# In a seven-level state recurrence, the key half of each level is scaled and copied ahead of the level's products

## The chip, the cores and the metric

The kernel runs on one core of a Trainium2 chip. The metric is the device time of one execution in microseconds (us), as the median of several runs. Five engines work side by side, each through its own queue of instructions in order: TensorE (PE, matrix products), VectorE (DVE), ScalarE (ACT), GpSimd (POOL) and SyncE (SP, which issues the loads). They wait for one another through semaphores only.

## The reference

One sequence of 256 tokens with 2048 features goes through two blocks. The first is a gated linear recurrence with input and output projections. The second mixes a convolution branch and a bidirectional gated state recurrence ("hgrn") and ends in an MLP. The change lies in the recurrence of the second block:

```python
def hgrn_chunk_scan(q, k, v, logf, s0):
    ...
    def step(s, xs):
        qc, kc, vc, gc = xs
        a = jnp.cumsum(gc, axis=2)
        a_last = a[:, :, -1:, :]
        inter = jnp.einsum('bhtk,bhkv->bhtv', qc * jnp.exp(a), s)
        diff = a[:, :, :, None, :] - a[:, :, None, :, :]
        decay = jnp.exp(jnp.where(tri[:, :, None], diff, -jnp.inf))
        scores = jnp.einsum('bhtk,bhsk,bhtsk->bhts', qc, kc, decay)
        intra = jnp.einsum('bhts,bhsv->bhtv', scores, vc)
        ...

def hgrn_bidir(q, v, gf, gb, s0f, s0b):
    o_f, s_f = hgrn_chunk_scan(q, gf[1], v, gf[0], s0f)
    fl = lambda t: jnp.flip(t, axis=1)
    o_b, s_b = hgrn_chunk_scan(fl(q), fl(gb[1]), fl(v), fl(gb[0]), s0b)
    return o_f + fl(o_b), s_f, s_b
```

So the output of token t is a sum over tokens s of (q_t times k_s times the product of the forget gates between s and t) times v_s, forwards and backwards, plus what comes from the start states `s_f` and `s_b`. There are 8 heads of 128 features. The start states come from a context of another 256 tokens (`hgrn_final_state`).

## The kernel before

**The stream of products.** All large projections are one long list of products of 128x128 weight tiles with 256 tokens. A weight block in float32 (`WF`, 128x1024) is loaded by SP into one of seven buffers; ACT copies it, rounded, to `WH` (`high`, L1031), DVE subtracts to get the rest `WL` (`low_part`, L1402). PE makes three matmuls for each weight tile (WH by high part, WH by low part, WL by high part); such a group of three is called a triple below. A block holds 8 triples. A projection tile of 16 triples is a `linear` of two halves; those of `pw` and `hout` have one half of 8. When a tile ends, ACT (for some kinds DVE too) empties its PSUM bank, one of banks 0 to 3 (`evac`).

**The order.** `timetable` (L56) writes the order of all work by hand into one list, `steps`, that every engine walks through in the same order. Smaller work runs in the background: `tick` calls `step` once in every `stride` triples, which is 4 from the stage `cv` on, and `step` issues the next part of the first name in the list `background` and of the first in `beside`. A part is what stands between two `yield`s of the function of that name, on each engine. From the stage `q` on the list is `conv_split`, `ctx_decayed`, `ctx_states`, then `hgrn` 0 to 3 (27 parts each); `beside` holds `readout` 0 to 3 (7 parts). Readout n starts when hgrn n is at its last part, so it runs beside the first levels of hgrn n+1. The stages on PE are then q, g, pw, gc, hout, gh, wout.

**ctx_states** (L907 on PE, L1276 on ACT) makes the start states, one head after the other: PE transposes into banks 4 and 5 (L918), ACT copies to `TK`, PE multiplies into bank 6, ACT copies to `S0` (`ctx_c`).

**hgrn** (L931 on PE, L1290 on ACT, L1764 on DVE) takes two heads at a time. `kf`, `kb` are keys, `qf`, `qb` queries for the two directions, `XK` is a pair of buffers that hold an interleaved copy of the keys. PE first transposes the values (L939) and makes a diagonal product of `KD` (after `hg_k`). Then follow seven levels, m = 1, 2, 4 to 64. For level L, before the change:

- ACT copies the even blocks of `kf` and the odd blocks of `kb` to `XK[L % 2]` and raises `hg_xk`; for L > 0 it waits for `hg_lv`.
- PE multiplies `XK[L % 2]` with the queries (4 matmuls, 8 in the trace), one part later, and raises `hg_pt`.
- DVE makes the totals of the next level out of this one's (two small multiplications), waits for `hg_pt`, scales `qf`, `kf`, `qb`, `kb` (four multiplications of 256 elements; the last raises `hg_lv`), and copies the masked product to `SS`.

Three parts, so 12 triples, lie between the products of two levels on PE. ACT's copies for the next level are one part ahead of its products; DVE's scalings two parts ahead.

**readout** (L989, L1323, L1822): ACT squares the output, PE sums with `ONES` into bank 7 (`stat`), ACT takes a square root (`root`), DVE the reciprocal (`inverse`, L1472), then DVE multiplies with norm and gate, ACT copies to `OH` and DVE subtracts to get the low part of it. The reciprocal stands in DVE's queue right behind the totals of level 0 of the next hgrn and ahead of the scalings of that level.

`Once.wait_ge` drops a wait that the same engine has already made.

Of the kernel before, what the change touches and what calls it, by code (L numbers as in the profile page):

```python
# [55 lines left out]
def timetable():  # L56
# [307 lines left out]
    for kind, j in order:  # L364
# [14 lines left out]
        elif kind == "gates":  # L379
            for b in range(2):  # L380
                begin()
                for ri in range(2):
                    for n in range(2):
                        new_tile((kind, (j, b, ri, n)))
                        product((kind, (j, b, ri, n), 0), 2)
                        evac((kind, (j, b, ri, n)))
                end()
            background.append(("recurrence", j))
        elif kind == "gate":
            if ("recurrence", (j - 16) // 4) not in finished:  # L390
                finish()
            linear(kind, j - 16)
        elif kind == "aout":
            if first:
                finish()
                steps.append(("warm", 1))
                steps.append(("split_p",))
            linear(kind, j)
        elif kind == "plep":
            begin()  # L400
            for n in range(4):
                new_tile((kind, 4 * j + n))
                product((kind, 4 * j + n, 0), 2)
                evac((kind, 4 * j + n))
            end()
            if first:
                steps.append(("stat", "y1"))
        elif kind == "pleg":
            if quad:
                prepare(fill=8)  # L410
                linear_quad(kind, j)
            else:
                linear(kind, j)
            if j == 5:
                steps.append(("load_ctx",))
            if j == 15:
                steps.append(("warm", 2))
        elif kind == "cv":
            if quad:
                mods_done(0, 8)  # L420
                steps.append(("gains", "mix"))
                prepare(fill=1, ahead=1)
                steps.append(("stat", "x2"))
                prepare(fill=3, ahead=1)
                linear_quad(kind, j)
                st["stride"] = 4
            else:
                linear(kind, j)
            if quad:
                steps.append(("keep",))  # L430
                background.append(("prepare_ctx", 0))
        elif kind == "cg":
            linear(kind, j - 48)
        elif kind == "i":
            if first:
                finish()
                background.append(("conv_branch", 0))
            linear(kind, j)
        elif kind == "ff":
            linear(kind, j - 8)  # L440
        elif kind == "fb":
            if first:
                while background:
                    step()
                background.append(("ctx_decayed", 0))
            linear(kind, j - 16)
        elif kind == "q":
            if first:
                finish()
                background += [("conv_split", 0), ("ctx_decayed", 1), ("ctx_states", 0)]  # L450
                background += [("hgrn", pr) for pr in range(4)]
                beside += [("readout", pr) for pr in range(4)]
            linear(kind, j - 24)
        elif kind == "g":
            if first:
                while ("ctx_states", 0) not in finished:
                    step()
            linear(kind, j - 32)
        elif kind in ("pw", "hout"):
            if kind == "hout" and first:  # L460
                finish()
            linear(kind, j, 1)
        elif kind in ("gc", "gh"):
            linear(kind, j - (56 if kind == "gc" else 72))
            if kind == "gh" and first:
                steps.append(("back",))
        elif kind == "wout":
            if first:
                mods_done(8, 12)
                steps.append(("gains", "wout"))  # L470
                steps.append(("warm", 3))
            linear(kind, j)
        elif kind == "mlp1":
            if quad:
                steps.append(("stat", "y2"))
                prepare(fill=3)
                for k in range(4):
                    steps.append(("add_y2", k))
                    steps.append(("sum_x3", k))
                    if k == 0:  # L480
                        prepare(fill=1, ahead=-2)
                mods_done(12, 20)
                steps.append(("gains", "mlp"))
                steps.append(("recip", "x3"))
                linear_quad(kind, j)
            else:
                linear(kind, j)
        elif kind == "mlp2":
            if j == (3, 0):
                mods_done(20, 24)  # L490
                steps.append(("gains", "out"))
            linear(kind, j)
# [22 lines left out]
def build(nc, ctx, ins, out):  # L515
# [7 lines left out]
    def sem(name):  # L523
# [38 lines left out]
    cx_a, cx_v, cb_v, cb_a, co_ok, cs_hi, cs_lo, k_ok = (  # L562
        sem(n) for n in ("cx_a", "cx_v", "cb_v", "cb_a", "co_ok", "cs_hi", "cs_lo", "k_ok"))
    ctx_t, ctx_a, ctx_s, ctx_c = (sem(n) for n in ("ctx_t", "ctx_a", "ctx_s", "ctx_c"))
    hg_k, hg_vt, hg_va, hg_dg, hg_sd, hg_xk, hg_pt, hg_lv, hg_sp, hg_of, hg_so, hg_qq, hg_ot, hg_o = (
        sem(n) for n in ("hg_k", "hg_vt", "hg_va", "hg_dg", "hg_sd", "hg_xk", "hg_pt", "hg_lv", "hg_sp", "hg_of",
                         "hg_so", "hg_qq", "hg_ot", "hg_o"))
    ro_a, ro_v, oh_hi, oh_lo = (sem(n) for n in ("ro_a", "ro_v", "oh_hi", "oh_lo"))
    sg_a, sg_v, gated_v = sem("sg_a"), sem("sg_v"), sem("gated_v")
# [193 lines left out]
    def tensor_program(tensor):  # L763
# [167 lines left out]
        def hgrn(pr):  # L931
# [18 lines left out]
            for level in range(7):  # L950
                m = 1 << level
                bk, xk = 5 - level % 2, XK[level % 2]
                yield
                w.wait_ge(hg_xk, 7 * pr + level + 1)
                w.wait_ge(hg_sp, 7 * pr + level - 1)
                if level == 0:
                    w.wait_ge(hg_sp, 7 * pr)
# [59 lines left out]
    def scalar_program(scalar):  # L1017
# [272 lines left out]
        def hgrn(pr):  # L1290
# [8 lines left out]
            for level in range(7):  # L1299
# [4 lines left out]
                    w.wait_ge(hg_k, pr + 1)  # L1304
                    w.wait_ge(hg_pt, 7 * pr)
                else:
                    w.wait_ge(hg_lv, 7 * pr + level)
                    w.wait_ge(hg_pt, 7 * pr + level - 1)
                act(even, blocks_of(kf, m)[:, :, 0, :], ACT.Copy)
                act(odd, blocks_of(kb, m)[:, :, 1, :], ACT.Copy).then_inc(hg_xk, 1)  # L1310
                yield
# [67 lines left out]
    def vector_program(vector):  # L1379
# [384 lines left out]
        def hgrn(pr):  # L1764
# [14 lines left out]
            for level in range(7):  # L1779
# [9 lines left out]
                    w.wait_ge(hg_lv, 7 * pr + level)  # L1789
                tt(nf, totals(tf)[:, :, 0], totals(tf)[:, :, 1], ALU.mult)  # L1790
                mark(tt(nb, totals(tb)[:, :, 0], totals(tb)[:, :, 1], ALU.mult))
                yield
                w.wait_ge(hg_pt, 7 * pr + level + 1)
                x = blocks_of(qf, m)[:, :, 1, :]
                tt(x, x, spread(tf, 0, m), ALU.mult)
                x = blocks_of(kf, m)[:, :, 0, :]
                tt(x, x, spread(tf, 1, m), ALU.mult)
                x = blocks_of(qb, m)[:, :, 0, :]
                tt(x, x, spread(tb, 1, m), ALU.mult)
                x = blocks_of(kb, m)[:, :, 1, :]  # L1800
                marked()
                tt(x, x, spread(tb, 0, m), ALU.mult).then_inc(hg_lv, 1)
                if level == 0:
                    w.wait_ge(hg_sd, pr + 1)
                else:
# [186 lines left out]
```

## Time and profile before

| what | value |
|---|---|
| median of 3 runs | 2200.4 us (2198.29 to 2200.71) |
| the profiled execution, its own time | 2203.85 us |
| its span | 2202.1 us |
| PE busy | 2134.1 us, 97% |
| DVE busy | 1586.3 us, 72% |
| ACT busy | 1006.8 us, 46% |

The span runs from the first to the last instruction of the profiled execution. An engine that is busy need not be the one that sets the end; but here PE's queue is occupied nearly all of the time. PE's idle time is what other engines can cost. In the trace L767 is the helper that issues all matmuls, L1385 the one for DVE's `tensor_tensor`, L1392 for its `scalar_tensor_tensor`, L1023 and L1024 those for ACT; so instructions are told apart by shape and place.

### The profile page before, as it was taken

Reading aid. Unit: us, or ns where it says so; the run is one execution under the profiler, and the core shown is the slowest. Engines: PE = TensorE matmul, PEld = TensorE weight load, DVE = VectorE, ACT = ScalarE, POOL = GpSimd, SP = SyncE. Lnnn points to the kernel's source line nnn. Section 1 sums busy time; section 2 is a strip of 40 time slices with the busy share of each in tenths; the row PEclk is TensorE's granted clock in tenths of the full one; section 3 lists DMA queues with packets and bytes.
Section 4 is the critical chain, followed back from the end, with each engine's and each line's share of the span. In section 5 each row is a group of like instructions: output and inputs, shape, how many; then the busy total and the mean of one; then the engine's idle time right before and its main releaser. Section 6 shows DMA issues by size and latency. Waiting matters only on the chain.

```text
span 2202.1 us, 34105 instructions
## 1 busy us (share of the span) xinstructions
PE 2134.1 (97%) x14048; PEld 1910.2 (87%) x14048; DVE 1586.3 (72%) x2365; ACT 1006.8 (46%) x1494; POOL 64.1 (3%) x61
## 2 busy tenths in 40 slices
PE   6999999999999999999999999989999999999997
PEld 5877899798988888999999999968888888888885
DVE  6757788588879876567777788776766766656655
ACT  5667444455632322445544444444444434434443
POOL 0000002020000000000000000100000000000011
PEclk9999999999999999999999999999999999999998
DMA  6556777676743466434436988936775675555552
GB/s 227 192 185 203 247 233 274 211 259 210 252 140 124 131 222 240 143 120 127 131 125 198 350 290 297 326 125 199 249 255 185 220 240 192 180 191 191 183 181 87
DMA packets 121691, 447.96 MB, mean 203 GB/s; under 512 B 13504, under 2 KB 13760, under 8 KB 121152
## 3 DMA queue, kind: packets, MB, share of 16 engines
q1 hardware_dynamic: 121536, 445.78, 60.1%
q8 instruction: 111, 1.82, 0.3%
q14 instruction: 44, 0.36, 0.1%
HBM read 441.53 MB, written 4.19 MB: 202 GB/s over the span
## 4 chain that ended last, share of the span: by engine, by line
PE 68%; DVE 4%; ACT 1%; issue 0%; DVEq 0%; ACTq 0%
PE bank L767 67%; DVE AR L1385 1%; DVE WL L1385 1%; DVE AR L1472 1%; DVE AR L1392 1%; DVE SR L1392 0%; PE bank L887 0%; ACT AR L1024 0%; ACT AR L1023 0%; ACT L1024 0%; PE bank L918 0%; ACT WH L1023 0%; ACT SR L1024 0%; DVE SR L1385 0%; ACT SR L1023 0%
## 5 line engine op out<-in xcount | busy, mean ns | idle before, releaser
L767 PE MATMUL bank<-SR,WH 128*128 128x256 f32 (+1 forms) x8128 | 1945.8, 325 | 29.1 <-DVE WL L1385 10.4
L767 PEld LDWEIGHTS bank<-SR,WH 128*128 128x128 f32 x8128 | 1363.5, 191 | 184.6 <-issue 31.0
L767 PE MATMUL bank<-SR,WL 128*128 128x256 f32 (+1 forms) x5088 | 1479.9, 291 | 0.0
L767 PEld LDWEIGHTS bank<-SR,WL 128*128 128x128 f32 x5088 | 972.5, 191 | 14.9
L1385 DVE TENSOR_TENSOR WL<-WF,WH 128x1024 fp32r<-128x1024 f32 x636 | 772.0, 1225 | 218.5 <-ACT WH L1023 218.0
L1023 ACT ACTIVATE WH<-WF 128x1024 fp32r<-128x1024 f32 x636 | 670.7, 1057 | 489.8 <-PE bank L767 448.8
L1392 DVE SCALAR_TENSOR_TENSOR AR<-WF,SM,AR 128x512 f32<-128x512 f32 x345 | 252.3, 752 | 8.7 <-DVE AR L1392 0.9
L1385 DVE TENSOR_TENSOR AR<-AR 128x256 f32<-128x256 f32 (+7 forms) x376 | 167.1, 477 | 60.4 <-ACT AR L1024 37.7
L1023 ACT ACTIVATE AR<-bank 128x256 f32<-128x256 f32 (+2 forms) x199 | 79.8, 415 | 240.1 <-PE bank L767 230.3
L1385 DVE TENSOR_TENSOR AR<-AR,bank 128x256 f32<-128x256 f32 x112 | 47.2, 421 | 120.0 <-PE bank L767 92.6
L1024 ACT ACTIVATE AR<-bank 128x256 f32<-128x256 f32 x152 | 55.7, 380 | 164.0 <-PE bank L767 163.7
L1911 POOL TENSOR_TENSOR AR<-AR 128x256 f32<-128x256 f32 x56 | 63.7, 1137 | 2116.6 <-ACT AR L1024 2116.4
L1023 ACT ACTIVATE SR<-AR 128x256 fp32r<-128x256 f32 (+1 forms) x154 | 62.9, 419 | 102.7 <-DVE AR L1385 83.3
L1385 DVE TENSOR_TENSOR SR<-AR,SR 128x256 fp32r<-128x256 f32 (+1 forms) x154 | 65.6, 435 | 28.0 <-ACT SR L1023 27.4
L1024 ACT ACTIVATE AR<-AR 128x256 f32<-128x256 f32 (+3 forms) x70 | 43.0, 615 | 87.6 <-DVE AR L1385 64.1
L1392 DVE SCALAR_TENSOR_TENSOR AR<-AR,PR 128x256 f32<-128x256 f32 (+12 forms) x168 | 73.8, 442 | 4.8
L767 PE MATMUL bank<-AR 128*128 128x128 f32 (+1 forms) x416 | 65.3, 300 | 9.5 <-ACT AR L1023 8.9
L767 PE MATMUL bank<-WF,SM 128*2 128x512 f32 x160 | 74.3, 601 | 0.0
L767 PEld LDWEIGHTS bank<-AR 128*128 128x128 f32 x416 | 56.9, 194 | 12.4 <-ACT AR L1023 10.4
L1385 DVE TENSOR_TENSOR AR<-bank,AR 128x256 f32<-128x256 f32 x80 | 33.6, 419 | 28.5 <-ACT AR L1024 21.1
L1472 DVE RECIPROCAL AR<-AR 128x256 f32<-128x256 f32 (+1 forms) x12 | 27.4, 2285 | 28.5 <-ACT AR L1024 28.5
L767 PEld LDWEIGHTS bank<-WF,SM 128*2 128x2 f32 x160 | 11.5, 85 | 41.4 <-issue 38.6
(64 smaller groups left out, 463.6 us busy)
## 6 DMA issues: line engine op xcount, KB each, us to landing
WF<-in_mlp SPq DMA_DIRECT2D x256, 512.0 KB, 4.5
WF<-in_mod SPq DMA_DIRECT2D x192, 512.0 KB, 4.8
WF<-in_w_in SPq DMA_DIRECT2D x176, 512.0 KB, 4.3
WF<-in_a_in SPq DMA_DIRECT2D x64, 512.0 KB, 4.9
WF<-in_a_out SPq DMA_DIRECT2D x32, 512.0 KB, 5.5
WF<-in_ple_g SPq DMA_DIRECT2D x32, 512.0 KB, 5.2
WF<-in_w_out SPq DMA_DIRECT2D x32, 512.0 KB, 5.6
WF<-in_pw SPq DMA_DIRECT2D x16, 512.0 KB, 3.6
```

The costliest lines, as they stand in the source:

```text
L767: return tensor.matmul(o, l, r, start=start, stop=stop, skip_group_check=True)
L1023: return scalar.activation(o, x, f, scale=scale)
L1024: return scalar.activation(o, x, f, scale=scale, bias=bias)
L1385: return vector.tensor_tensor(o, a, b, op)
L1392: return vector.scalar_tensor_tensor(o, a, s, b, op1, op2)
L1472: vector.reciprocal(dst, dst).then_inc(st_rs, 1)
L1911: pool.tensor_tensor(ACC, ACC, SQ[ft % 2], ALU.add).then_inc(acc, 1)
```

## The change

In the levels, DVE scales the keys in the part of the totals, one part earlier than the queries, as soon as ACT has copied them (`hg_xk`), and raises a new semaphore `hg_kv`. ACT's copies of the next level wait for `hg_kv`, no longer for `hg_lv`. PE's products of a level now wait for `hg_lv` themselves, since the queries may be scaled after the copy of the keys. DVE's query scalings keep their wait for the products (`hg_pt`). No instruction is added or removed in a level. Apart from that, `ctx_states` is no longer run to its end ahead of the first `g` tile; its last parts and all that follows them in the background come at their usual distance of 4 triples.

```diff
@@ timetable
         elif kind == "g":
-            if first:
-                while ("ctx_states", 0) not in finished:
-                    step()
             linear(kind, j - 32)
@@ tensor_program, hgrn
                 w.wait_ge(hg_xk, 7 * pr + level + 1)
+                if level:
+                    w.wait_ge(hg_lv, 7 * pr + level)
                 w.wait_ge(hg_sp, 7 * pr + level - 1)
@@ scalar_program, hgrn
                 else:
-                    w.wait_ge(hg_lv, 7 * pr + level)
+                    w.wait_ge(hg_kv, 7 * pr + level)
                     w.wait_ge(hg_pt, 7 * pr + level - 1)
+                if level == 1:
+                    w.wait_ge(hg_dg, pr + 1)
                 act(even, blocks_of(kf, m)[:, :, 0, :], ACT.Copy)
                 act(odd, blocks_of(kb, m)[:, :, 1, :], ACT.Copy).then_inc(hg_xk, 1)
@@ vector_program, hgrn
                 mark(tt(nb, totals(tb)[:, :, 0], totals(tb)[:, :, 1], ALU.mult))
+                w.wait_ge(hg_xk, 7 * pr + level + 1)
+                x = blocks_of(kf, m)[:, :, 0, :]
+                tt(x, x, spread(tf, 1, m), ALU.mult)
+                x = blocks_of(kb, m)[:, :, 1, :]
+                tt(x, x, spread(tb, 0, m), ALU.mult).then_inc(hg_kv, 1)
                 yield
                 w.wait_ge(hg_pt, 7 * pr + level + 1)
                 x = blocks_of(qf, m)[:, :, 1, :]
                 tt(x, x, spread(tf, 0, m), ALU.mult)
-                x = blocks_of(kf, m)[:, :, 0, :]
-                tt(x, x, spread(tf, 1, m), ALU.mult)
                 x = blocks_of(qb, m)[:, :, 0, :]
-                tt(x, x, spread(tb, 1, m), ALU.mult)
-                x = blocks_of(kb, m)[:, :, 1, :]
                 marked()
-                tt(x, x, spread(tb, 0, m), ALU.mult).then_inc(hg_lv, 1)
+                tt(x, x, spread(tb, 1, m), ALU.mult).then_inc(hg_lv, 1)
```

PE's queue of the kernel before, where the stage `q` ends: the last context head but one is multiplied, then head 7 is transposed (L918) and multiplied with nothing in between, then come the values of hgrn 0 (L939), and only then the first `g` tile, in bank 0.

```order
L767 MATMUL bank6<-AR 128x128 [waits ctx_c,ctx_a]
L767 MATMUL bank6<-AR 128x128 x3
L918 MATMUL bank4<-CN,AR 128x128 x2
L918 MATMUL bank5<-CN,AR 128x128
L918 MATMUL bank4<-CN,AR 128x128 x2
L918 MATMUL bank5<-CN,AR 128x128
L767 MATMUL bank6<-AR 128x128 [waits ctx_c,ctx_a]
L767 MATMUL bank6<-AR 128x128 x3
L939 MATMUL bank6<-CN,AR 128x128 [waits ctx_c]
L939 MATMUL bank6<-CN,AR 128x128 x3
L767 MATMUL bank0<-SR,WH 128x256 [waits free0,w_lo]
```

The same place in the changed kernel (line numbers of that file; rows of `g` triples left out at the dots).

```order
L764 MATMUL bank6<-AR 128x128 [waits ctx_c,ctx_a]
L764 MATMUL bank6<-AR 128x128 x3
L764 MATMUL bank0<-SR,WH 128x256 [waits free0,w_lo]
...
L915 MATMUL bank4<-CN,AR 128x128 x2
...
L764 MATMUL bank6<-AR 128x128 [waits ctx_c,ctx_a]
L764 MATMUL bank6<-AR 128x128 x3
L764 MATMUL bank0<-SR,WH 128x256 [waits w_lo]
...
L936 MATMUL bank6<-CN,AR 128x128 [waits ctx_c]
```

Four triples now stand between each of these steps, and the whole background from here on comes three parts (12 triples) later against the stream of tiles.

DVE's queue of the kernel before at the reciprocal of readout 0, beside hgrn 1. 128x256 rows are totals or scalings of level 0; 128x128 ones the totals of level 1 and 128x128x2 ones its scalings.

```order
L1385 TENSOR_TENSOR AR<-AR 128x256 [waits hg_k]
L1385 TENSOR_TENSOR AR<-AR 128x256
L1472 RECIPROCAL AR<-AR 128x512 [waits st_sq]
L1385 TENSOR_TENSOR WL<-WF,WH 128x1024 [waits w_hi]
L1385 TENSOR_TENSOR AR<-AR 128x256 [waits hg_pt]
L1385 TENSOR_TENSOR AR<-AR 128x256 x2
L1385 TENSOR_TENSOR AR<-AR 128x256 [waits v_own]
...
L1392 SCALAR_TENSOR_TENSOR AR<-bank3,AR 128x256 [waits sg_a]
...
L1385 TENSOR_TENSOR AR<-AR 128x128x2 [waits hg_pt]
L1385 TENSOR_TENSOR AR<-AR 128x128x2 x2
L1385 TENSOR_TENSOR AR<-AR 128x128x2 [waits v_own]
```

The same in the changed kernel.

```order
L1386 TENSOR_TENSOR AR<-AR 128x256 [waits hg_k]
L1386 TENSOR_TENSOR AR<-AR 128x256
L1386 TENSOR_TENSOR AR<-AR 128x256 [waits hg_xk]
L1386 TENSOR_TENSOR AR<-AR 128x256
L1473 RECIPROCAL AR<-AR 128x512 [waits st_sq]
L1386 TENSOR_TENSOR AR<-AR 128x256 [waits hg_pt]
L1386 TENSOR_TENSOR AR<-AR 128x256 [waits v_own]
...
L1386 TENSOR_TENSOR AR<-AR 128x128x2 [waits hg_xk]
L1386 TENSOR_TENSOR AR<-AR 128x128x2
L1386 TENSOR_TENSOR WL<-WF,WH 128x1024 [waits w_hi]
L1386 TENSOR_TENSOR AR<-AR 128x128x2 [waits hg_pt]
L1386 TENSOR_TENSOR AR<-AR 128x128x2 [waits v_own]
```

The key scalings of level 0 have moved ahead of the reciprocal, and those of level 1 stay between it and the query scalings of level 1. The gate multiplication of a `g` tile (bank3) is no longer in this stretch, since the readout now lies in the stage `pw`.

ACT's queue of the kernel before at the root of readout 1 (bank7).

```order
L1023 ACTIVATE AR<-AR 128x256 [waits hg_pt,hg_k]
L1023 ACTIVATE AR<-AR 128x256
L1023 ACTIVATE AR<-bank3 128x256 [waits prod]
L1023 ACTIVATE WH<-WF 128x1024 [waits landed4]
L1024 ACT_TABLE_LOAD
L1024 ACTIVATE AR<-bank7,CN 128x512 [waits st_mm]
```

The same root in the changed kernel.

```order
L1022 ACTIVATE AR<-bank0 128x256 [waits prod]
L1022 ACTIVATE WH<-WF 128x1024 [waits landed5]
L1022 ACTIVATE AR<-AR 128x256 [waits hg_pt,hg_k]
L1022 ACTIVATE AR<-AR 128x256
L1023 ACTIVATE AR<-bank7,CN 128x512 [waits st_mm]
```

The table load ahead of this root is gone: between the roots of readout 0 and 1 there is no sigmoid any more. ACT's queue has two table loads less in all; SP's and POOL's queues are as before.

## Rows read from the trace of the kernel before

**Rows 1.** The page's part 1: busy us, share of the span, instructions.
```profile
PE 2134.1 (97%) x14048; PEld 1910.2 (87%) x14048; DVE 1586.3 (72%) x2365; ACT 1006.8 (46%) x1494; POOL 64.1 (3%) x61
```

**Rows 2.** Windows of 100 us: length, busy of PE, PEld, DVE, ACT, POOL, clock, DMA.
```profile
900.00:1000.00 100.00, 97.98 (x812) 96.92 (x811) 64.53 (x117) 47.10 (x83) 0.00 (x0) 1.00 0.43 141
1000.00:1100.00 100.00, 94.58 (x749) 92.38 (x748) 76.04 (x145) 53.06 (x91) 0.00 (x0) 0.98 0.40 125
1100.00:1200.00 100.00, 97.47 (x778) 95.26 (x778) 71.26 (x121) 48.30 (x74) 0.00 (x0) 1.00 0.45 147
1200.00:1300.00 100.00, 100.00 (x837) 100.00 (x836) 84.69 (x112) 45.97 (x68) 0.00 (x0) 1.00 0.91 324
```

**Rows 3.** Waits of PE from 940 to 1300 us: total us, times, longest.
```profile
PE bank L767 <- ACT AR L1023: 8.9, 7, 1.8
PE bank L767 <- DVE AR L1385: 0.6, 1, 0.6
PE bank L939 <- ACT AR L1023: 0.5, 1, 0.5
```

**Rows 4.** Timeline of PE: start, us, instructions [idle before <-releaser].
```profile
948.14 1.16 PE L767 MATMUL bank<-AR 128*128 128x128 f32 x8 [0.96 <-ACT AR L1023]
949.77 0.65 PE L939 MATMUL bank<-CN,AR 128*128 128x128 f32 x4 [0.47 <-ACT AR L1023]
952.45 1.16 PE L767 MATMUL bank<-AR 128*128 128x128 f32 x8 [0.58 <-DVE AR L1385]
1016.00 2.03 PE L767 MATMUL bank<-AR 128*128 128x128 f32 x8 [1.81 <-ACT AR L1023]
1023.88 1.16 PE L767 MATMUL bank<-AR 128*128 128x128 f32 x8 [0.84 <-ACT AR L1023]
1071.91 1.23 PE L767 MATMUL bank<-AR 128*128 128x128 f32 x8 [0.95 <-ACT AR L1023]
1079.27 1.16 PE L767 MATMUL bank<-AR 128*128 128x128 f32 x8 [1.82 <-ACT AR L1023]
1127.84 1.23 PE L767 MATMUL bank<-AR 128*128 128x128 f32 x8 [1.51 <-ACT AR L1023]
1134.39 0.82 PE L767 MATMUL bank<-AR 128*128 128x128 f32 x5 [1.02 <-ACT AR L1023]
```

**Rows 5.** Windows, PE alone: length, busy, granted clock, DMA.
```profile
1016.00:1018.00 2.00, 2.00 (x9) 0.52 0.45 184
1018.00:1020.00 2.00, 2.00 (x13) 0.63 0.00 0
1080.00:1082.00 2.00, 2.00 (x19) 1.00 0.42 111
```

**Rows 6.** Timeline of PE: two triples in a row.
```profile
1020.00 0.40 PE L767 MATMUL bank<-SR,WH 128*128 128x256 f32 x2
...
1020.36 0.40 PE L767 MATMUL bank<-SR,WH 128*128 128x256 f32 x2
```

**Rows 7.** Timeline of DVE beside readout 1 and levels 0 and 1.
```profile
1066.44 3.35 DVE L1472 RECIPROCAL AR<-AR 128x512 f32<-128x512 f32 x1 [2.86 <-ACT AR L1024]
1069.71 1.36 DVE L1385 TENSOR_TENSOR AR<-AR 128x256 f32<-128x256 f32 x4
...
1077.03 1.43 DVE L1385 TENSOR_TENSOR AR<-AR 128x256 f32<-128x256 f32 x4
```

**Rows 8.** Timeline of ACT: the table load ahead of readout 1's root.
```profile
1064.42 1.28 ACT L1024 ACT_TABLE_LOAD   x1
```

**Rows 9.** Timeline of DVE beside readout 2.
```profile
1121.23 3.35 DVE L1472 RECIPROCAL AR<-AR 128x512 f32<-128x512 f32 x1 [4.51 <-ACT AR L1024]
...
1131.42 2.16 DVE L1385 TENSOR_TENSOR AR<-AR 128x256 f32<-128x256 f32 x7
```

**Rows 10.** Timeline of DVE: the reciprocal of readout 0.
```profile
1009.40 3.35 DVE L1472 RECIPROCAL AR<-AR 128x512 f32<-128x512 f32 x1 [1.39 <-ACT AR L1024]
```

More of the change, by code:

```diff
@@ L564, in build @@
     ctx_t, ctx_a, ctx_s, ctx_c = (sem(n) for n in ("ctx_t", "ctx_a", "ctx_s", "ctx_c"))
-    hg_k, hg_vt, hg_va, hg_dg, hg_sd, hg_xk, hg_pt, hg_lv, hg_sp, hg_of, hg_so, hg_qq, hg_ot, hg_o = (
-        sem(n) for n in ("hg_k", "hg_vt", "hg_va", "hg_dg", "hg_sd", "hg_xk", "hg_pt", "hg_lv", "hg_sp", "hg_of",
+    hg_k, hg_vt, hg_va, hg_dg, hg_sd, hg_xk, hg_pt, hg_kv, hg_lv, hg_sp, hg_of, hg_so, hg_qq, hg_ot, hg_o = (
+        sem(n) for n in ("hg_k", "hg_vt", "hg_va", "hg_dg", "hg_sd", "hg_xk", "hg_pt", "hg_kv", "hg_lv", "hg_sp", "hg_of",
                          "hg_so", "hg_qq", "hg_ot", "hg_o"))
```

## The prediction

> **What bounds the kernel now.** I read the shares first: PE is busy 2134.1 of 2202.1 us [rows 1], so only its idle time and its clock are to be had. Then the windows: of the 300 us from 900 to 1200, where q, g, pw and gc run with the background, PE loses 2.0, 5.4 and 2.5 us, 10 in all, and from 1200 to 1300 nothing [rows 2]. The view of waits puts that down to ten us in nine waits, eight of them on a copy of ACT [rows 3]. The timeline places them [rows 4]: three lie at the end of ctx_states and the start of hgrn 0 (0.96 + 0.47 + 0.58 = 2.01 us), and six are products of level 1 or 2 in hgrn 1, 2 and 3, in pairs: 1.81 and 0.84, 0.95 and 1.82, 1.51 and 1.02, together 7.95 us. No level above 2, and none of hgrn 0, which has no readout beside it, waits. So levels as such keep up with PE; what is late is a level that has a readout's reciprocal in DVE's queue, 3.35 us each [rows 7, 9, 10].
>
> PE's clock adds to this once. Behind the wait of 1.81 us the granted clock is 0.52 for two us and 0.63 for two more, which is the lower of its two levels (1.2 GHz) most of the way, and costs 2 x 0.48 + 2 x 0.37 = 1.7 us of work [rows 5]. Behind the wait of 1.82 us it is 1.00 [rows 5]. All that can be won in this stretch is 9.96 + 1.7 = 11.7 us.
>
> **How far a pair of waits can shrink.** In each pair the end is set by one chain through DVE: reciprocal, scalings of level 0, the readout's own work, totals and scalings of level 1, ACT's copies, products of level 2. PE's wait before level 1 is only an advance on that: if it goes and the chain stays, PE waits longer before level 2. So a pair must be costed as a whole, against the chain. For readout 1, level 2 would be due without any wait at 1079.27 - 1.82 - 0.95 = 1076.50; DVE ends its last scaling at 1077.03 + 1.43 = 1078.46, and PE starts 0.81 later [rows 4, 7]. The clock's 1.7 us behind the first wait of readout 0 is covered in the same way: had it not been lost, level 2 would have waited for 0.84 + 1.7. So that pair stands for 4.35 us, the others for 2.77 and 2.53.
>
> **What the change takes from that chain.** First, the two key scalings of level 0 now stand ahead of the reciprocal, where DVE has been idle for 1.39, 2.86 and 4.51 us [rows 7, 9, 10]; that takes two of four scalings of 1.43 us, 0.71, off the chain. (If that cover were gone they would cost 0.71 again.) The key scalings of level 1 do not leave it: they stand ahead of its query scalings, behind the reciprocal. Second, PE no longer waits for ACT's copies, which now follow key scalings that lie a part earlier, but directly for the query scaling: of the 0.81 us between DVE and PE some 0.04 (an estimate: a hand-over between engines) stays, 0.77 goes. Together 1.48 us for each pair. Before level 1 this is more than 0.95, so that wait ends; PE then comes to level 2 with nothing lost.
>
> **What the shift by three parts does.** It changes what lies beside each readout, which I took from the queues.
> - Readout 0 now stands at the end of g, where readout 1 stood against a tile's start, with the same work around it on DVE and ACT; I use the times of readout 1. Level 2 is due at 1076.50, ready at 1078.46 - 0.71 + 0.04 = 1077.79: a wait of 1.29 stays of 4.35. Gain 3.06.
> - Readout 1 stands as readout 2 did, without a table load ahead of its root (1.28 us [rows 8]) and without one gate multiplication (a quarter of 1.43 us, 0.36). With the times of readout 2, due is 1134.39 - 1.02 - 1.51 = 1131.86, ready 1134.39 - 0.71 - 0.77 - 0.36 = 1132.55 without the table load's help [rows 4, 9]. It needs 0.69 of 1.28 us to have no wait left, and I take it to have that. Gain all of 2.77; 2.08 at the least.
> - Readout 2 stands as readout 1 did, but at a half of a tile: one evacuation less ahead of the root, and one gate multiplication more on DVE, about equal. A wait of 1.3 stays of 2.53. Gain 1.2.
>
> That is 7.0 us. Work is the same in number, apart from two table loads less on ACT (1.28 each), an engine at 46% [rows 1], which cost nothing of themselves.
>
> **ctx_states no longer forced.** Four triples, 4 x 0.36 = 1.44 us [rows 6], now lie between each of the steps that followed at once. That is more than each of the three waits 0.96, 0.47 and 0.58, and PE had none such for heads 0 to 6, which run at that distance. I take all 2.01; bounds are 0 (if the copies stand behind a weight copy on ACT) and 2.01. The last readout ends 12 triples, 4.3 us, later; the forced finish ahead of hout is 11 parts away now, 44 triples, so it is not met.
>
> **The sum.** 3.06 + 2.77 + 1.2 + 2.0 = 9.0 us. From 1135 us on PE does not wait for long in gc and hout [rows 2], so a gain there is carried to the end. The profiled execution took 2203.85 us; that would become 2194.8. The median shown is 3.45 us below it, and from it I get 2200.4 - 9.0 = 2191.4 us. What a measurement of this kernel can tell from no change is about 0.2%, 4.4 us.
>
> The edit has a new wait: DVE waits for `hg_xk` ahead of its key scalings, and behind it in its queue stand the next `WL` and the query scalings, for which PE waits. ACT has made these copies a part, 1.44 us, earlier in the order, so the wait should be short except right behind an evacuation.
>
> **The clock and the skill.** The trace shows one fall of the clock behind nine waits, and none behind the wait of 1.82 us. The Trainium skill (TensorE: Matmul & The Clock Gate, "HAM oscillation — how this bites in real kernels") says that a PE which waits inside its loop is set back to half rate, so that the work behind the wait runs cold. By it the two waits that I leave could bring falls with them; by the trace mostly not. It makes a rival below, worked from rows.
>
> **The rivals.**
> - All waits go: my chains are too long by 1.3 us, since a table load less or a shorter queue on ACT pulls the root forward. 11.7 us, 2188.7. For it: DVE is idle ahead of every reciprocal, so the root sets the start. Against: nothing ahead of the root of readout 0 or 2 got shorter. 0.10.
> - The clock falls behind each of the two waits that stay, before level 2, with no wait behind them to hide it: 2 x 1.7 = 3.4 lost, gain 5.6, 2194.8. For it: the one fall behind 1.81. Against: 1.82 without one. 0.12.
> - The change does little: DVE's new wait pushes the query scalings back as far as the keys moved forward, and only ACT's hop is saved, 3 x 0.77 = 2.3, with 2.0 of ctx_states: 4.3 us, 2196.1, about the bound of measurement. 0.14.
> - Slower: DVE, at 76% in the busiest window [rows 2], waits in every level until ACT has got past an evacuation and a weight copy, and hands that on to PE: 28 levels x 0.81 = 22.7 less 9.0, 2214. It decides once DVE reaches a level's query scalings more than 12 triples, 4.3 us, behind the products of the level before. Against it: no level without a readout waits now, though its chain has one engine more in it. 0.06.
> - My forecast, 7 to 11 us: 0.58.
>
> **How the numbers follow.** The likeliest is 2191.4. The range goes from all waits gone, 2188.5, to a little past the third rival, 2196.5; about 0.1 is left out above (the slow one and part of the third) and some below. Faster holds the forecast and the first two rivals, 0.80; same the third, 0.14; slower 0.06.
>
> **What would show it.** Right: PE shows no wait at head 7 and at hgrn 0; before level 1 no wait beside any readout; before level 2 a wait of some 1.3 us beside readouts 0 and 2, with DVE named as the releaser, and none beside readout 1; the scalings there come as two and two. PE's busy time per triple is as now. Wrong: waits of PE for `WL`, or for DVE in levels without a readout; DVE idle with ACT's copy as releaser ahead of key scalings; or a clock below 1.00 behind what is left. A change in stages before 940 or past 1200 us would be none of mine.

## The result, and the profile after

The changed kernel takes 2187.0 us in the median of 5 runs (2186.13 to 2190.06), the one before, run beside it, 2198.29 us (2196.83 to 2200.71). The ratio is 0.9949, 95% interval 0.9935 to 0.9964: faster by 11.3 us, 0.51%, where 9.0 us and a time of 2191.4 had been forecast; 2188.5 was the low end of the range, so the time lies below it. Later runs of the same kernel gave ratios of 0.9963 (0.9951 to 0.9975) and 0.9950 (0.9933 to 0.9966).

Part 1 of the changed kernel's page answers to [rows 1].

```profile
PE 2124.7 (97%) x14048; PEld 1907.8 (87%) x14048; DVE 1585.0 (73%) x2365; ACT 1003.4 (46%) x1492; POOL 64.3 (3%) x61
```

Its windows answer to [rows 2] (length; busy us of PE, PEld, DVE, ACT and POOL; granted clock; DMA share; GB/s).

```profile
900.00:1000.00 100.00, 100.00 (x837) 99.66 (x837) 64.73 (x117) 47.87 (x86) 0.00 (x0) 1.00 0.45 144
1000.00:1100.00 100.00, 98.28 (x793) 96.38 (x792) 80.20 (x153) 51.58 (x91) 0.00 (x0) 1.00 0.43 137
1100.00:1200.00 100.00, 98.22 (x786) 96.24 (x785) 75.43 (x124) 50.20 (x76) 0.00 (x0) 1.00 0.47 155
```

From 900 to 1000 us PE has no gap left, and in the next two windows it loses 1.7 and 1.8 us instead of 5.4 and 2.5. The timeline of PE has two waits where [rows 4] had nine; both are products of level 2, beside readouts 0 and 2.

```profile
1023.04 1.13 PE L764 MATMUL bank<-AR 128*128 128x128 f32 x8 [1.66 <-issue]
1129.56 1.13 PE L764 MATMUL bank<-AR 128*128 128x128 f32 x8 [1.78 <-issue]
```

The profile names no releaser for them ("issue"). DVE's timeline beside readout 0 does: the last line ends at 1022.95, PE starts at 1023.04.

```profile
1010.11 1.42 DVE L1386 TENSOR_TENSOR AR<-AR 128x256 f32<-128x256 f32 x4
1011.59 3.35 DVE L1473 RECIPROCAL AR<-AR 128x512 f32<-128x512 f32 x1
1014.86 0.69 DVE L1386 TENSOR_TENSOR AR<-AR 128x256 f32<-128x256 f32 x2
...
1019.97 1.16 DVE L1386 TENSOR_TENSOR AR<-AR 128x128 f32<-128x128 f32 x4
1021.05 1.22 DVE L1386 TENSOR_TENSOR WL<-WF,WH 128x1024 fp32r<-128x1024 f32 x1
1022.19 0.76 DVE L1386 TENSOR_TENSOR AR<-AR 128x256 f32<-128x256 f32 x2
```

The four multiplications ahead of the reciprocal are totals and key scalings of level 0, the two behind it the query scalings, which were four in [rows 7]. Beside readout 1 PE waits for nothing. DVE still waits for ACT there, 3.13 us, but now ahead of the key scalings, for ACT's copy of the keys; the root is ready by the time they are done, so the reciprocal itself is not held up.

```profile
1063.26 0.76 DVE L1386 TENSOR_TENSOR AR<-AR 128x256 f32<-128x256 f32 x2 [3.13 <-ACT AR L1022]
1063.93 3.35 DVE L1473 RECIPROCAL AR<-AR 128x512 f32<-128x512 f32 x1
...
1073.45 1.83 DVE L1386 TENSOR_TENSOR AR<-AR 128x128 f32<-128x128 f32 x6
```

**Where the time came from.** The transposes that close a modulation column group (L887 of the kernel before, L884 of the changed one) are landmarks in PE's queue: the same instructions at the same place among the products in both kernels. First the kernel before, then the changed one.

```profile
851.05 0.60 PE L887 MATMUL bank<-CN,AR 128*128 128x128 f32 x4
1193.06 0.60 PE L887 MATMUL bank<-CN,AR 128*128 128x128 f32 x4
1745.48 0.60 PE L887 MATMUL bank<-CN,AR 128*128 128x128 f32 x4
2093.59 0.60 PE L887 MATMUL bank<-CN,AR 128*128 128x128 f32 x4
```

```profile
851.33 0.60 PE L884 MATMUL bank<-CN,AR 128*128 128x128 f32 x4
1183.88 0.60 PE L884 MATMUL bank<-CN,AR 128*128 128x128 f32 x4
1736.02 0.60 PE L884 MATMUL bank<-CN,AR 128*128 128x128 f32 x4
2077.59 0.60 PE L884 MATMUL bank<-CN,AR 128*128 128x128 f32 x4
```

The stretch that holds the change, from 851 to behind gc, went from 342.01 to 332.55 us: 9.46 us. From there to 1740 the two differ by 0.28 us (552.42 and 552.14). The last stretch, in the MLP, which the change doesn't touch, went from 348.11 to 341.57 us: 6.54 us more. The two spans, 2202.1 and 2186.1 us, differ by 16.0, about the sum of both. The difference of the medians, 11.3 us, lies between 9.46 and 16.0. So there were two questions for the experiments: does the 9.46 come from the chain that the prediction described, and whose are the 6.54?

### The profile page after: what moved, and what is told of

It reads as the page before. It is cut to its first block, busy times and chain, and to the rows that moved or that the text cites. A ratio compares the mean times of both kernels' runs of the same rounds, so it can differ in the third digit from the quotient of the medians.

```text
span 2186.1 us, 34103 instructions
## 1 busy us (share of the span) xinstructions
PE 2124.7 (97%) x14048; PEld 1907.8 (87%) x14048; DVE 1585.0 (73%) x2365; ACT 1003.4 (46%) x1492; POOL 64.3 (3%) x61
## 3 DMA queue, kind: packets, MB, share of 16 engines
q8 instruction: 111, 1.82, 0.3%
## 4 chain that ended last, share of the span: by engine, by line
PE 68%; DVE 4%; ACT 1%; issue 1%; DVEq 0%; ACTq 0%
PE bank L764 68%; DVE AR L1386 1%; DVE AR L1473 1%; DVE AR L1393 1%; DVE WL L1386 1%; DVE SR L1393 0%; PE bank L884 0%; PE bank L915 0%; ACT AR L1023 0%; ACT L1023 0%; ACT AR L1022 0%; ACT WH L1022 0%; DVE SR L1386 0%; ACT SR L1023 0%; ACT SR L1022 0%
## 5 line engine op out<-in xcount | busy, mean ns | idle before, releaser
L1386 DVE TENSOR_TENSOR AR<-AR 128x256 f32<-128x256 f32 (+6 forms) x376 | 166.7, 474 | 59.3 <-ACT AR L1023 37.9
```

The source lines that it names most:

```text
L1386: return vector.tensor_tensor(o, a, b, op)
```

## The experiments

Each was timed beside the kernel before. Below, "stretch" is the time between the first two landmarks, and "MLP stretch" that between the last two. A "fall" is a fall of PE's granted clock to about half for a few us.

**1. The levels alone.** The changed kernel with the forced end of ctx_states put back.

```diff
         elif kind == "g":
+            if first:
+                while ("ctx_states", 0) not in finished:
+                    step()
             linear(kind, j - 32)
```

> The changed kernel with the forced end of ctx_states put back, so only the order inside the levels is new. Chain theory: the three waits at head 7 and hgrn 0 (2.0 us) are back as before; each pair of waits beside a readout is 1.48 us smaller than before, whatever its size, so 3 x 1.48 = 4.4 us gain, and the waits that stay are before level 2 (about 1.3 us beside readout 1, about 1.0 beside readout 2, up to 2.9 beside readout 0). Rival (the copies of ACT were the wait): all six level waits go, a gain of 8 us or more. Transposes of the first column group behind gc (1193.06 us in the trace of before, 1183.88 in that of the changed kernel) at about 1188.5 by the first, at 1185 by the rival. Time from there to the end: as in other runs within the few us by which the pace of PE differs from run to run.

2196.32 us (2193.45 to 2200.83), before 2198.85 (2196.39 to 2206.32, 28 runs for this and the next three), ratio 0.9987 (0.9977 to 0.9998). The stretch is 339.45 us, a gain of 2.56, not 4.4. The three waits at head 7 and hgrn 0 are back (0.96, 0.47 and 0.59 us). The timeline of PE beside the readouts:

```profile
1015.38 1.20 PE L767 MATMUL bank<-AR 128*128 128x128 f32 x8 [0.40 <-issue]
1023.33 1.67 PE L767 MATMUL bank<-AR 128*128 128x128 f32 x8 [2.44 <-ACT AR L1025]
1078.85 1.13 PE L767 MATMUL bank<-AR 128*128 128x128 f32 x8 [1.65 <-issue]
1132.61 1.16 PE L767 MATMUL bank<-AR 128*128 128x128 f32 x8 [1.11 <-ACT AR L1025]
```

Each readout keeps the wait that the chain asks for: 2.84, 1.65 and 1.11 us, where 2.9, 1.3 and 1.0 were expected. Most of what is missing is the clock. The windows of PE behind the 2.44 us:

```profile
1023.00:1025.00 2.00, 1.67 (x9) 0.70 0.57 227
1025.00:1027.00 2.00, 2.00 (x12) 0.50 0.39 82
1027.00:1029.00 2.00, 2.00 (x18) 0.95 0.88 221
```

Here it falls behind level 2, where no later wait covers it; in the trace of before it fell behind level 1 and was covered. Experiment 7 measures what this costs, 1.5 us; without it the gain would be 4.0 (an estimate, 2.56 + 1.5).

**2. The shift alone.** The kernel before, with only the forced end of ctx_states taken out.

```diff
         elif kind == "g":
-            if first:
-                while ("ctx_states", 0) not in finished:
-                    step()
             linear(kind, j - 32)
```

> The kernel before with only the forced end of ctx_states taken out. Chain theory: the three early waits go (2.0 us); readout 0 gets the surroundings that readout 1 had (4.35 to 2.77, gain 1.6), readout 1 those of readout 2 without a table load and a gate multiplication (gain 1.8), readout 2 those of readout 1 (loss 0.2): 5.2 us in all, transposes behind gc at about 1187.9 us. The waits beside the readouts are still before levels 1 and 2 both, on ACT's copies. Rival (the shift only takes the three early waits): gain 2.0, transposes at 1191.

2192.81 us (2190.41 to 2198.23), ratio 0.9976 (0.9967 to 0.9984). The stretch is 336.58 us, 5.43 less than before. No wait at head 7 or hgrn 0 is left, and the timeline of PE has the pairs

```profile
1015.98 1.23 PE L764 MATMUL bank<-AR 128*128 128x128 f32 x8 [0.95 <-ACT AR L1020]
1023.32 1.16 PE L764 MATMUL bank<-AR 128*128 128x128 f32 x8 [1.81 <-ACT AR L1020]
1070.75 1.23 PE L764 MATMUL bank<-AR 128*128 128x128 f32 x8 [0.36 <-ACT AR L1020]
1076.97 1.16 PE L764 MATMUL bank<-AR 128*128 128x128 f32 x8 [0.68 <-ACT AR L1020]
1124.78 1.23 PE L764 MATMUL bank<-AR 128*128 128x128 f32 x8 [0.74 <-ACT AR L1020]
1132.47 1.16 PE L764 MATMUL bank<-AR 128*128 128x128 f32 x8 [2.15 <-ACT AR L1020]
```

The sums are 2.76, 1.04 and 2.89 us: readout 0 has what readout 1 had (0.95 and 1.82) to 0.01 us, readout 1 has less than readout 2 had (2.53), readout 2 a little more than readout 1 had (2.77). The part of the change that looks like housekeeping brought more than half of the gain. With the 4.0 of experiment 1 that makes 9.4 us, so the two parts add up to the 9.46 of the whole, though the 4.0 is an estimate.

DVE's timeline, the reciprocals of readouts 0 and 1:

```profile
1010.50 3.35 DVE L1469 RECIPROCAL AR<-AR 128x512 f32<-128x512 f32 x1 [0.72 <-ACT AR L1021]
...
1064.13 3.35 DVE L1469 RECIPROCAL AR<-AR 128x512 f32<-128x512 f32 x1 [3.70 <-ACT AR L1021]
```

The idle 0.72 us ahead of the first is the room that two key scalings (0.71) have there with the shift. The forecast, going by the times of readout 1, took it to be 2.86. It just suffices.

**3. The readout's closing work two parts later.** In the changed kernel, `readout` has 9 parts instead of 7; the new ones lie between the reciprocal and the closing work, on every engine alike.

```diff
             inverse(f"ro{pr}")
-            yield
-            yield
+            for _ in range(4):
+                yield
             w.wait_ge(st_rs, RECIP[f"ro{pr}"])
```

> The changed kernel with the closing work of each readout (norm, gate, high and low parts) two parts later than before, so behind the query scalings of level 1 in DVE's queue. Chain theory: 0.87 + 0.69 + 0.48 + 0.76 = 2.8 us leave the chain from the reciprocal to the products of level 2, more than the waits of 1.66 and 1.78 us that the changed kernel has there; both go, transposes behind gc at 1183.9 - 3.4 = 1180.5 us and 3.4 us less in all. Rival (what is late is the subtraction WL, or the reciprocal alone): the waits stay above 1 us, or move to level 3 in the same size.

2194.47 us (2189.62 to 2199.04), ratio 0.9980 (0.9971 to 0.9990). The rival had waits of over 1 us staying, for another reason; that they would grow stood in neither. The stretch is 337.28 us, 4.7 more than in the changed kernel, and PE waits longer than there (6.8 us, not 3.44), all on ACT:

```profile
PE bank L764 <- ACT AR L1022: 6.8, 3, 2.5
```

DVE did what was wanted; ACT didn't. Beside readout 0, DVE's timeline, then ACT's:

```profile
1019.77 0.75 DVE L1386 TENSOR_TENSOR AR<-AR 128x256 f32<-128x256 f32 x2
...
1021.07 0.87 DVE L1393 SCALAR_TENSOR_TENSOR AR<-AR,PR 128x256 f32<-128x256 f32 x2
1021.97 0.69 DVE L1386 TENSOR_TENSOR AR<-AR 128x512 f32<-128x512 f32 x1
```

```profile
1022.69 0.72 ACT L1022 ACTIVATE SR<-AR 128x256 fp32r<-128x256 f32 x2 [4.87 <-DVE AR L1386]
1023.32 0.71 ACT L1022 ACTIVATE AR<-AR 128x256 f32<-128x256 f32 x2
```

DVE ends the query scalings of level 1 at 1020.52, before they are due. But ACT's copies of the high parts (`SR`) wait for DVE's closing work, which ends at 1022.66, and the key copies of level 2 stand behind them in ACT's queue. They end at 1024.03, and PE starts at 1024.08. Of the 4.7 us some 1.5 are no wait but a fall behind this wait of 2.35 us (clock 0.69, 0.50 and 0.95 in the three windows of 2 us from 1023), at the price that experiment 7 measures.

**4. The changed kernel again.** No edit.

> The changed kernel unaltered. Of the 16.0 us by which its first traced execution is shorter, 9.5 lie before the transposes behind gc and 6.5 behind 1740 us, where a pair of products takes 0.345 us in it and 0.352 in that of before. Pace theory: this second part is not of the change; this trace shows it at another place or not at all, and the transposes behind gc again at 1183.9 us, within 0.5. Rival (the change does something to the MLP): the pair takes 0.345 us from 1736 us on in this trace too.

2189.39 us (2187.32 to 2194.62), ratio 0.9963 (0.9951 to 0.9975). The stretch is 332.54 us (332.55 in the first trace) with waits of 1.66 and 1.78 us, so the trace repeats to 0.01 us there. The MLP stretch is 341.57 us again, which by itself speaks for the rival; experiment 8 decides.

**5. The closing work three parts later.** As 3, with 10 parts.

```diff
             inverse(f"ro{pr}")
-            yield
-            yield
+            for _ in range(5):
+                yield
             w.wait_ge(st_rs, RECIP[f"ro{pr}"])
```

> The changed kernel with the closing work of each readout three parts later (two in the run before). With two parts the query scalings of level 1 were early enough, but ACT's high parts, which wait for DVE's closing work, stood in its queue ahead of the key copies of level 2. With three they stand behind them. Chain theory with ACT's queue counted: the waits before level 2 (1.66 and 1.78 us in the changed kernel) go, no new one comes, transposes from 850 to behind gc 332.5 - 3.5 = 329.0 us apart, total 3.4 us under the changed kernel. Rival (the work only moves on): waits of 1 to 2.5 us appear before level 3, on DVE or on ACT's copies.

2190.95 us (2188.42 to 2191.75) beside 2203.36 (2198.55 to 2204.56, 15 runs for this and the next two), ratio 0.9948 (0.9934 to 0.9962). The stretch is 328.68 us, 3.87 less than in the changed kernel, and PE has no wait in it. Experiment 9 has this kernel's rows.

**6. Keys scaled early, copied late.** The changed kernel, with the wait of ACT's copies as before.

```diff
                 else:
-                    w.wait_ge(hg_kv, 7 * pr + level)
+                    w.wait_ge(hg_lv, 7 * pr + level)
```

> The changed kernel, but ACT's copies of a level wait for hg_lv (query scalings) as in the kernel before, so the keys are scaled early and yet copied late. It leaves the first term (0.71 us of key scalings ahead of the reciprocal) and takes the second away (0.77 us, ACT's hop). Chain theory: each wait before level 2 is 0.77 us longer: 2.43 beside readout 0, 0.6 beside readout 1 (0.15 us of slack there now), 2.55 beside readout 2, 2.2 us more in all, and up to 1.7 more if the clock falls behind the first; stretch of 334.7 to 336.5 us. Rival (only the hop mattered, or only the scalings): 2.9 us or more on top of 3.44 beside each readout, or no difference to the changed kernel (332.5).

2194.77 us (2190.89 to 2196.19), ratio 0.9963 (0.9950 to 0.9976). The stretch is 336.22 us, within what was expected, 3.7 more than in the changed kernel. The timeline of PE:

```profile
1015.08 1.23 PE L764 MATMUL bank<-AR 128*128 128x128 f32 x8 [0.28 <-ACT AR L1022]
1022.45 1.16 PE L764 MATMUL bank<-AR 128*128 128x128 f32 x8 [1.82 <-ACT AR L1022]
1075.52 1.16 PE L764 MATMUL bank<-AR 128*128 128x128 f32 x8 [0.66 <-ACT AR L1022]
1130.36 1.60 PE L764 MATMUL bank<-AR 128*128 128x128 f32 x8 [2.16 <-ACT AR L1022]
```

The waits are 4.92 us in all, 1.5 more than 3.44 and not 2.2. From the products of level 0 to those of level 2 beside readout 0 PE takes 13.45 us here (1009.00 to 1022.45) and 12.74 in experiment 4 (1009.71 to 1022.45): 0.71 more, which is the hop through ACT, of which only 0.44 is booked as waiting. So a wait costs some 0.2 to 0.3 us beyond what its brackets say. Experiment 2 differs from this one, as far as this way goes, only by the key scalings, which there still stand behind the reciprocal, and takes 14.09 us over the same way (1009.23 to 1023.32). So the key scalings are worth 0.64 us, the hop 0.71, and both together 1.35. Behind the wait of 2.16 us the clock fell (0.73, 0.50 and 0.92 in the three windows of 2 us from 1130), which is most of what is left.

**7. The kernel before again.** No edit.

> The kernel before, unaltered, for a second trace. Pace theory: the stretch from the transposes near 850 us to those behind gc is 342.0 us again, within 0.3, with the same nine waits; and the stretch between the transposes near 1745 and near 2090 us is either 348.1 or 341.6 us, as in all traces so far, with a time of the execution near 2204 or near 2197. In the second case the lower pace belongs to the execution and not to the kernel. Rival: it is 348.1 us again and the kernel before cannot take the other pace.

2203.31 us (2199.86 to 2205.82, 11 runs), ratio 1.0006 (0.9998 to 1.0015). The MLP stretch is 348.12 us, as its rival had it: the kernel before was not seen at the lower value in either trace. That some of its executions have it is likely (2203.85 less 6.54 is 2197.3, amid the 2196.83 to 2200.71 of its runs beside the result) but not shown. The stretch is 343.49 us, not 342.0, and the difference measures the clock. The timeline of PE, and its windows behind the second line:

```profile
1016.22 1.23 PE L767 MATMUL bank<-AR 128*128 128x128 f32 x8 [1.81 <-ACT AR L1023]
1024.11 1.16 PE L767 MATMUL bank<-AR 128*128 128x128 f32 x8 [2.35 <-ACT AR L1023]
```

```profile
1024.00:1026.00 2.00, 1.89 (x13) 0.81 0.26 107
1026.00:1028.00 2.00, 2.00 (x12) 0.50 0.87 252
1028.00:1030.00 2.00, 2.00 (x16) 0.83 0.75 236
```

In the first trace of before the clock fell behind level 1 and level 2 waited 0.84 us [rows 4, 5]. Here it held, and level 2 waited 2.35: it begins 7.89 us after level 1 here and 7.88 us there. So the slow clock inside the chain cost nothing. Then it fell behind level 2, and the stretch is 1.48 us longer.

**8 and 9. The changed kernel and the late readout on one chip.** No edit to the changed kernel and to that of experiment 5.

> The changed kernel again, beside the one with the late readout on the same chip. Stretch from the transposes near 850 us to those behind gc 332.5 us, waits of 1.66 and 1.78 us. Its time against the kernel before: 9.5 us less, a ratio of 0.9957.

> The changed kernel with the readout's closing work three parts later, again, beside the changed one on the same chip. Stretch of 328.7 us, no wait; its time 3.9 us under that of the changed kernel and 13.3 under that of before, ratio 0.9939. Rival: the chip's own differences between executions hide it, and the two cannot be told apart.

The changed kernel: 2190.53 us (2189.06 to 2194.2), ratio 0.9950 (0.9933 to 0.9966). The late readout: 2186.79 us (2185.69 to 2192.06), ratio 0.9936 (0.9920 to 0.9952). Before: 2203.49 (2196.0 to 2205.41, 11 runs for these two and the next). The stretches are 332.58 and 328.68 us. The medians differ by 3.7 us where the stretches differ by 3.9; the two intervals overlap, so by whole times alone it isn't settled, but the stretch is: 328.68 us in both traces of the late readout, 332.54 to 332.58 in three of the changed kernel.

ACT's timeline of the late readout: the key copies of level 2 now stand ahead of the high parts.

```profile
1019.20 0.73 ACT L1022 ACTIVATE AR<-AR 128x256 f32<-128x256 f32 x2 [0.92 <-DVE AR L1386]
1023.14 0.72 ACT L1022 ACTIVATE SR<-AR 128x256 fp32r<-128x256 f32 x2 [3.22 <-DVE AR L1386]
```

The landmarks of the changed kernel here:

```profile
850.83 0.60 PE L884 MATMUL bank<-CN,AR 128*128 128x128 f32 x4
1183.41 0.60 PE L884 MATMUL bank<-CN,AR 128*128 128x128 f32 x4
1735.04 0.60 PE L884 MATMUL bank<-CN,AR 128*128 128x128 f32 x4
2083.14 0.60 PE L884 MATMUL bank<-CN,AR 128*128 128x128 f32 x4
```

Its MLP stretch is 348.10 us, with 341.57 in its two earlier traces. That answers the second question as far as it goes: the same kernel has both values, so the 6.54 us are not of the change. But this trace is of another chip than that of experiment 4 (the chip of the first is not known), and no kernel was traced at both values on one chip, so whether the value belongs to the chip or to the execution is open. The chip alone doesn't set it: experiments 1 to 4 ran on one chip, and 3 had 348.11, the others 341.57.

**10. More transposes.** The late readout, with

```diff
                 w.wait_ge(mod_v, mod_blocks(cg))
+                if cg >= 21:
+                    for x in range(4):
+                        tensor.transpose(bank[4][:, x * P:x * P + P], MA[v][:, x * P:x * P + P], ident)
                 for x in range(4):
```

> The late readout, with each of the last three closings of a modulation column group (the transposes near 1593, 1735 and 2077 us) making four transposes more, into a bank that nothing reads. In all traces the pace of PE in the MLP changes only at such a group: 348.1 or 341.6 us between the last two. If the pace is set anew by each group of transposes, the stretches behind them (141.8 us always so far, 348.1 or 341.6) take another value or flip in some of them, by 2 to 7 us; the transposes alone cost 4 x 0.06 x 3 = 0.8 us. Rival (the pace belongs to the chip or the execution): the stretch between the last two is what the other two kernels show on this chip, plus 0.3 us.

2188.46 us (2185.84 to 2189.87), ratio 0.9938 (0.9923 to 0.9953). The stretches behind the three groups are as in experiments 5 and 9 but for the transposes themselves (0.43 us a group). In this trace four more transposes did not change the pace of PE.

## Why the prediction missed, point by point

- **What bounds the kernel, and the chain.** Right. What limits a level beside a readout is the chain through DVE to the products of level 2: experiment 1 takes part of it away and keeps the rest as one wait, experiment 7 shows the clock's fall inside it to be free (7.88 and 7.89 us from level 1 to level 2 with and without it), and in the kernel of experiments 5 and 9, where the closing work leaves it, the waits are gone.
- **The two terms, 0.71 and 0.77.** Right within a tenth: experiments 2 and 6 put them at 0.64 and 0.71, together 1.35 for the 1.48 forecast. That the first came out whole beside readout 0 was partly luck, since its room was 0.72 us and not 2.86. What stays in the changed kernel, at the places forecast, was 1.29, 0 and 1.3 us and is 1.66, 0 and 1.78. For readout 0, DVE needs 8.01 us from the reciprocal's end to the last query scaling (1014.94 to 1022.95), 7.96 by the forecast; what was off is when level 2 is due, 6.44 us behind that end and not 6.71. In the times of before, PE had been slowed there by its wait ahead of level 1 beyond the idle time booked for it, and I had taken over that slowed time as the free one.
- **The shift.** Right, and the best part of the prediction: 5.2 us expected in experiment 2 after the fact, 5.43 measured, the pairs within 0.2 us of 2.77, 0.9 and 2.7. The table load that leaves readout 1 did what it was taken to do. Beside readout 2 of the kernel before, the reciprocal started 0.70 us behind the products of level 0; beside readout 1 it starts 0.46 us ahead of them in experiment 2 and 0.36 in the changed kernel. That is 1.16 and 1.06 us earlier, where 0.69 of the load's 1.28 were needed.
- **ctx_states, 2.01 us.** Right. The three waits are gone in experiment 2 and in the changed kernel, and back in experiment 1.
- **The sum, 9.0 us.** 9.46 in the stretch. Waits fell by 6.5 instead of 7.3 us, but each wait that goes takes some 0.2 us with it that is not booked as waiting. Seven of them and the clock's 1.5 give 6.5 + 1.4 + 1.5 = 9.4. The sum held because two errors nearly cancel, 0.8 us too much for the waits and 1.4 left out, which is luck.
- **How the numbers follow.** This is the step that failed. "The median shown is 3.45 us below it, and from it I get 2200.4 - 9.0" took one profiled execution and three runs as fixed points, and the range was made of mechanisms of the change alone: what executions and sets of runs of one kernel differ by was put at nothing, and a change past 1200 us was to be "none of mine". The 4.4 us between 2191.4 and 2187.0 are 2.1 of the base (with two more runs the median of the kernel before went from 2200.4 to 2198.29), 0.5 of the stretch (9.46 for 9.0) and 1.8 that stay open. With the stretch alone the time would have been 2190.9, inside the range. The same kernel before had medians of 2198.3, 2198.9, 2203.4 and 2203.5 us in four sets of runs, the changed one 2187.0, 2189.4 and 2190.5. The MLP stretch alone makes 6.5 us between two traces of one kernel. The open 1.8 us (2198.3 - 9.46 = 2188.8 against 2187.0) are within what single medians here differ by, and no run shows their cause. As the medians of the kernel before spread over 5.2 us, a range of 5 us to either side of 2191.4 would have been honest. The ratio forecast, 0.9959, lies inside all three measured intervals.
- **The rivals.** "All waits go" is nearest to the time but not what happened: two waits stayed. The clock falling behind a wait that stays did not happen in the three traces of the changed kernel, but did in experiments 1, 3, 6 and 7, at 1.5 us where it was measured (experiment 7). That the change does little, because DVE's new wait gives back what the key scalings won, is ruled out by their 0.64 us between experiments 2 and 6. The slower rival, DVE held by ACT in every level, did not occur: in no trace does PE wait in a level without a readout. One sign that the prediction named as speaking against it did appear, DVE idle ahead of key scalings with ACT's copy as releaser: 3.13 us beside readout 1 and some 0.75 us at one later level each of hgrn 1, 2 and 3. It cost PE nothing, since DVE has time to spare there; the sign was badly chosen.
- **The clock.** Of the waits of 1.8 us and more between 850 and 1200 us in all traces, thirteen, five had a fall behind them (1.81, 2.16, 2.35, 2.35 and 2.44 us) and eight had none (1.81 to 2.48); no shorter one had. Elsewhere, once the clock has first risen, each trace has four long waits, near 53, 151, 304 and 1450 us (2.30, 4.2 to 5.5, 2.67 and 4.5 us), and the clock fell at all of them in all twelve traces; "one fall" in the prediction counts this stretch alone. The Trainium skill (TensorE: Matmul & The Clock Gate, "HAM oscillation — how this bites in real kernels") ties such falls to waits in PE's loop that are long enough; the waits of its example are longer than any between 850 and 1200 us here. The prediction left that condition out when it cited the section. These traces agree that only the longer waits are followed by a fall, but a wait of 1.81 us can be, and one of 2.48 us need not be; where page and measurement differ, the measurement decides.

## What to carry to other kernels

Cost a pair of waits as one chain, from the instruction that starts it to the last product that needs it: in these traces an earlier wait, or a slow clock, inside the chain was only an advance on the later one. When work in one queue is moved later, look what its consumers in other queues now stand ahead of: two parts later cost 4.7 us here (some 1.5 of it a fall of the clock), three parts later brought 3.9, with DVE's order as wanted in both. A few us in 2200 are judged by landmarks of the trace on either side of the change, which repeat to hundredths of a us as long as the clock falls at the same places, and not by one median.

## What the runs showed of the hardware

- Identical products of PE run at one of two paces in the MLP. The stretch from the landmark near 1740 us to the last one takes 341.57 us in the traces of experiments 1, 2 and 4 and of the changed kernel, and 348.10 to 348.12 in all others but for experiment 10's extra transposes; no value lies between. The granted clock is 1.00 in both, and DVE and ACT take the same time for each instruction. The timelines show the 512-column product 0.40 us long in one and 0.39 in the other, and a pair of products starts 0.353 us after the pair ahead of it in one and 0.347 in the other. Traces of one kernel differ in it (experiments 4 and 8, on two chips). The one thing tried, more transposes, did not set it, and its cause stays open.
- A second stretch, from the small transposes (2x2) near 1470 us to the landmark near 1600, has such a pair of values too, 126.06 and 123.78 us; the second was seen only in experiments 5, 6, 9 and 10. The ratio is the same as in the MLP, 1.02, and no trace has the lower value in both, so the pace can change within one execution, either way. Here no kernel was seen with both values, so that the order of a kernel's instructions sets it is not ruled out. This too is open.
- A wait of PE costs more than the idle time that the profile books: 0.71 against 0.44 us in experiment 6, and 3.87 against 3.44 for the two waits that go in experiment 5, some 0.2 to 0.3 us for each wait.
